# Expert rows fetched one chunk early into the combine of a two-layer encoder; the last chunk's rows added by TensorE

## The reference

```
x = LN(ALPHA * x + Mix(x))      # conv module, windowed attention, gMLP; shared input and output projection
x = LN(ALPHA * x + MoE(x))      # 16 SwiGLU experts (1024 -> 512 -> 1024), top 2 of the best of 4 groups
```

```
for e in range(N_EXPERTS):
    he = silu(x2d @ w_gate[e]) * (x2d @ w_up[e])
    y = y + gates[:, e:e + 1] * (he @ w_down[e])
```

## Time and profile before

| what | value |
|---|---|
| median of 3 runs | 1137.98 us |
| profiled execution, its own time | 1142.18 us |
| its span in the trace | 1140.4 us |
| mean granted TensorE clock | 0.918 |
| busy: TensorE, VectorE, ScalarE, GpSimd | 965.8, 807.7, 648.9, 521.6 us |
| DMA moved | 268.99 MB |

### The profile page before, as it was taken

How to read it: one execution, slowest core, us unless ns; L and a number is a source line. 1 busy time by engine, 2 the same in 40 slices (tenths; PEclk the granted TensorE clock), 3 DMA queues, 4 the chain that set the end, 5 groups by cost and what they waited for, 6 DMA issues and landing times. The chain is left out here.

```text
span 1140.4 us, 15102 instructions
## 1 busy us (share of the span) xinstructions
PE 965.8 (85%) x4700; PEld 780.4 (68%) x4700; DVE 807.7 (71%) x964; ACT 648.9 (57%) x723; POOL 521.6 (46%) x297
## 2 busy tenths in 40 slices
PE   4998998289999999999269979982899999999950
PEld 3866775168888887878268757751688888888840
DVE  2996755567778787777467967555677787878737
ACT  4224712078878887877213347120788787878730
POOL 3435354035656556565205453440356565564621
PEclk9998998679999999999679989986799999999985
DMA  8521183079999999963713211930799999999625
GB/s 271 187 81 39 57 331 147 1 263 360 373 368 366 381 355 371 364 264 108 227 38 111 74 46 51 336 146 3 265 373 378 370 357 372 352 370 367 255 114 143
DMA packets 122511, 268.99 MB, mean 236 GB/s; under 512 B 10608, under 2 KB 26128, under 8 KB 121968
## 3 DMA queue, kind: packets, MB, share of 16 engines
q1 hardware_dynamic: 110192, 243.99, 59.0%
q0 software_dynamic: 12288, 24.60, 6.7%
HBM read 263.38 MB, written 24.64 MB: 253 GB/s over the span
## 5 line engine op out<-in xcount | busy, mean ns | idle before, releaser
L1500 POOL TENSOR_TENSOR wl<-w_down,wh 128x2048 fp32r<-128x2048 f32 x33 | 151.6, 4595 | 165.5 <-ACT wh L937 165.5
L1026 DVE TENSOR_TENSOR wl<-w_gate,wh 128x2048 fp32r<-128x2048 f32 x71 | 166.0, 2339 | 58.3 <-ACT wh L937 30.4
L1026 DVE TENSOR_TENSOR wl<-w_up,wh 128x2048 fp32r<-128x2048 f32 x66 | 151.2, 2293 | 29.5 <-ACT wh L937 29.1
L702 PE MATMUL bank<-wh,xTh 128*128 128x512 f32 x528 | 143.4, 394 | 4.5 <-ACT wh L937 4.5
L937 ACT ACTIVATE wh<-w_down 128x2048 fp32r<-128x2048 f32 x66 | 126.8, 1921 | 30.0 <-PE bank L702 30.0
L702 PE MATMUL bank<-wh,xTl 128*128 128x512 f32 x528 | 142.8, 393 | 0.0
L702 PE MATMUL bank<-wl,xTh 128*128 128x512 f32 x528 | 142.8, 393 | 0.0
L937 ACT ACTIVATE wh<-w_up 128x2048 fp32r<-128x2048 f32 x66 | 126.5, 1917 | 25.5 <-PE bank L720 24.9
L1444 POOL TENSOR_TENSOR wl<-w_gate,wh 128x2048 fp32r<-128x2048 f32 x17 | 78.0, 4593 | 135.5 <-ACT wh L794 135.2
L1026 DVE TENSOR_TENSOR xTl<-bank,xTh 128x512 fp32r<-128x512 f32 (+1 forms) x168 | 89.9, 574 | 62.5 <-ACT xTh L941 24.7
L396 PE MATMUL bank<-xTh,wh 128*128 128x512 f32 (+2 forms) x272 | 112.2, 412 | 24.9 <-DVE xTl L1026 21.1
(11 more groups left out here) (206 smaller groups left out, 1726.5 us busy)
## 6 DMA issues: line engine op xcount, KB each, us to landing
w_up<-in_exp_w_up SPq DMA_DIRECT2D x32, 2048.0 KB, 13.3
w_down<-in_exp_w_down SPq DMA_DIRECT2D x32, 2048.0 KB
w_gate<-in_exp_w_gate SPq DMA_DIRECT2D x32, 2048.0 KB, 12.6
w_gate<-in_w_in SPq DMA_DIRECT2D x14, 1024.0 KB, 5.5
w_gate<-in_w_out SPq DMA_DIRECT2D x8, 1024.0 KB, 5.0
x_rows<-xtok POOLq DMA_DIRECT2D x8, 512.0 KB, 3.0
w_gate<-in_rows_mix SPq DMA_DIRECT2D x2, 1536.0 KB, 6.3
w_up<-in_x_t SPq DMA_DIRECT2D x4, 512.0 KB, 7.5
```

The costliest lines, as they stand in the source:

```text
L702: mm = pe.matmul(bank[piece][:, :], xgT[m][:, 4 * (i % 2) + k, :], w[q][:, k, :], start=(i % 2 == 0 and n == 0 and k == 0), stop=(i % 2 == ...
L1026: return dve.tensor_tensor(out, src, high.bitcast(F32), ALU.subtract)
L1500: pool.tensor_tensor(wl[s][:, :], slot[r][p][:, cols], wh[s][:, :].bitcast(F32), ALU.subtract)\
```

## The change

- Both DRAM buffers `yd` are filled with zeros once: SP issues 16 stores of 512 KB from a zeroed tile (`zero_choices`) behind piece 9 of the first layer, and GpSimd waits for them before the first gather.
- The last chunk's result is not scattered. `load_choices` waits only for the scatter issued within the last chunk's iteration; rows that the last chunk would have written are read as zeros. It fetches both choices for tiles 0 and 1, and GpSimd adds the second choices of tiles 2 and 3 only. In the transition it stands ahead of the mixer's parameters on SP.
- VectorE builds a table of the last chunk (`hot_last`): for each slot of the chunk and each token of a tile, one where the slot's token is that token, else zero. It joins x and the fetched rows (`join`), and TensorE adds in PSUM the identity times the joined tile and the table times `ysb` (`add_choices`): per tile four plain float32 products of 128x128 by 128x512.
- The norm's statistics and its first product read PSUM (`norm_ffn`); the last product is done by ScalarE (scale) and GpSimd (shift) for tiles 0 and 2 in the transition and tiles 0 to 2 at the end, by VectorE for the others. GpSimd takes the power of tile j + 1 ahead of the shift of tile j.
- In the transition ScalarE makes the high parts of pieces 0 and 1 ahead of the last `result`, each as soon as its slot is free; the slots are shifted by one in the second layer so that the right ones are free. `turn` uses other banks and no longer waits for low parts.

The diff, cut to the changed lines and a little around them; left out are the declarations of semaphores, the further places where the slot index changes in the same way, and the rename of the call of `norm`:

```diff
@@ -158,6 +158,8 @@
         cve, crs = small[:, 36:40], small[:, 40:44]
+        last_tok = small[:, 44:45]
+        last_hot = sg
         bnm = [small[:, 112 + 12 * j:124 + 12 * j] for j in range(TT)]
@@ -259,7 +262,11 @@
-            return bank[4 + 2 * (j % 2) + i] if q % 2 else bank[4 * i + j]
+            return bank[2 * j + i] if q % 2 else bank[4 * i + j]
+        def shifted(l, ffn):
+            return (0, 2) if ffn and l + 1 < DEPTH else (0, 1, 2)
@@ -307,14 +314,21 @@
-                end = first_chunk(sp, l, E)
-                sp.wait_ge(split_done[1], end)
-                sp.wait_ge(split_done[2], end)
-                sp.wait_ge(scattered, (end + (l + 1)) * 16)
+                last, end = first_chunk(sp, l, E - 1), first_chunk(sp, l, E)
+                sp.wait_ge(scattered, end * 16)
+                sp.wait_ge(split_done[1], last)
+                sp.wait_ge(split_done[2], last)
                 y = yd[l].rearrange("(r j p) n -> j p r n", r=2, p=P)
                 for j in range(TT):
-                    n = 1 if j else 2
+                    n = 1 if j >= 2 else 2
                     sp.dma_start(ycomb[j][:, 0:n, :], y[j][:, 0:n, :]).then_inc(y_in[j], 16)
+            def zero_choices():
+                sp.wait_ge(pool_chain, 1)
+                for l in range(DEPTH):
+                    for r in range(8):
+                        sp.dma_start(yd[l][P * r:P * r + P, :], xg).then_inc(y_zeroed, 16)
@@ -334,13 +348,15 @@
                     load_piece(l, 1)
+                    load_choices(l - 1)
                     sp.wait_ge(split_done[2], first_chunk(sp, l - 1, E))
                     mix_params(l)
-                    load_choices(l - 1)
                 for q in range(2, PIECES):
...
                     load_piece(l, q)
+                    if q == 9 and l == 0:
+                        zero_choices()
                     if q == 4 and l == 0:
@@ -629,8 +645,6 @@
                 pe.wait_ge(ln_out, TT * q + j + 1)
-                if q % 2 and j >= 2:
-                    pe.wait_ge(tr_low, 2 * (TT * q + j - 1))
                 for k in range(KD):
@@ -742,6 +756,18 @@
                 narrow(l, c, 5)
+            def add_choices(l, j, end):
+                pe.wait_ge(xc_set, TT * l + j + 1)
+                for h in range(2):
+                    pe.matmul(bank[2 * j + h][:, :], ident, xtok[:, j, 512 * h:512 * h + 512], start=True, stop=False)
+                pe.wait_ge(last_set, l + 1)
+                pe.wait_ge(y_set, end + (l + 1))
+                for h in range(2):
+                    mm = pe.matmul(bank[2 * j + h][:, :], last_hot[:, P * j:P * j + P], ysb[:, 512 * h:512 * h + 512],
+                                   start=False, stop=True)
+                mm.then_inc(y_added, 1)
@@ -771,6 +797,9 @@
                     chunk(l, c)
+                end = first_chunk(pe, l, E)
+                for j in range(TT):
+                    add_choices(l, j, end)
@@ -996,14 +1025,24 @@
                     hidden_high(end, l, i)
+                if l + 1 < DEPTH:
+                    act.wait_ge(half_used, halves_done(end, 1, 1))
+                    piece(l + 1, 0)
+                    act.wait_ge(half_used, halves_done(end, 1, 1) + 1)
+                    piece(l + 1, 1)
                 result(end, l, 1)
                 if l + 1 < DEPTH:
-                    for n in range(2):
-                        piece(l + 1, n)
-                    for j in range(TT):
-                        columns_high(2 * l + 1, j)
+                    scaled(2 * l + 1, 0)
+                    columns_high(2 * l + 1, 0)
+                    columns_high(2 * l + 1, 1)
+                    scaled(2 * l + 1, 2)
+                    columns_high(2 * l + 1, 2)
+                    columns_high(2 * l + 1, 3)
                     piece(l + 1, 2)
+                else:
+                    for j in range(TT - 1):
+                        scaled(2 * l + 1, j)
@@ -1128,21 +1167,15 @@
                 dve.wait_ge(piece_high, n + 1)
-                low(wl[n % SLOTS][:, :], wraw[n % 2], wh[n % SLOTS][:, :]).then_inc(piece_low, 1)
+                low(wl[(n + l) % SLOTS][:, :], wraw[n % 2], wh[(n + l) % SLOTS][:, :]).then_inc(piece_low, 1)
...
-                    dve.wait_ge(y_in[j], 16 * (l + 1))
-                    if j:
-                        dve.wait_ge(y_joined[j - 1], 16 * (l + 1))
-                    link(dve.scalar_tensor_tensor(xtok[:, j, :], xtok[:, j, :], ALPHA, ycomb[j][:, 0, :],
-                                                  ALU.mult, ALU.add))
-                    if j == 0:
-                        link(dve.tensor_tensor(xtok[:, j, :], xtok[:, j, :], ycomb[0][:, 1, :], ALU.add))
-                    norm_stats([xtok[:, j, 0:512], xtok[:, j, 512:1024]], j, 2)
+                    dve.wait_ge(y_added, TT * l + j + 1)
+                    norm_stats([bank[2 * j][:, :], bank[2 * j + 1][:, :]], j, 2)
                 else:
@@ -1165,19 +1198,49 @@
-            def norm(l, ffn):
-                dve.wait_ge(rows_in, 32 * l + (32 if ffn else 16))
+            def join(l, j):
+                dve.wait_ge(y_in[j], 16 * (l + 1))
+                if j >= 2:
+                    dve.wait_ge(y_joined[j - 2], 16 * (l + 1))
+                x = dve.scalar_tensor_tensor(xtok[:, j, :], xtok[:, j, :], ALPHA, ycomb[j][:, 0, :], ALU.mult, ALU.add)
+                if j < 2:
+                    link(x)
+                    x = dve.tensor_tensor(xtok[:, j, :], xtok[:, j, :], ycomb[j][:, 1, :], ALU.add)
+                x.then_inc(xc_set, 1)
+            def hot_last(l):
+                at = dve.value_load(starti[0:1, bass.ds(l * (E + 1) + E, 1)], min_val=1, max_val=MAXCH - 1)
+                link(dve.tensor_copy(last_tok, toki[:, bass.ds(at - 1, 1)]))
+                iota = cst[:, K_IOTA:K_IOTA + P]
                 for j in range(TT):
-                    norm_in(l, j, ffn)
-                    if ffn and l + 1 < DEPTH and j >= 1:
-                        columns_low(2 * l + 1, j - 1)
+                    x = dve.tensor_scalar(last_hot[:, P * j:P * j + P], iota, float(P * j), last_tok,
+                                          ALU.add, ALU.is_equal)
+                x.then_inc(last_set, 1)
+            def norm_mix(l):
+                dve.wait_ge(rows_in, 32 * l + 16)
+                for j in range(TT):
+                    norm_in(l, j, 0)
                     dve.scalar_tensor_tensor(xtok[:, j, :], xtok[:, j, :], mv[:, 2 * j:2 * j + 1],
-                                             rows3[:, 0 if ffn else 1, :], ALU.subtract, ALU.mult).then_inc(ln_norm, 1)
-                    if ffn or j == TT - 1:
-                        norm_out(l, j, ffn)
-                    if not ffn and j >= 2:
+                                             rows3[:, 1, :], ALU.subtract, ALU.mult).then_inc(ln_norm, 1)
+                    if j == TT - 1:
+                        norm_out(l, j, 0)
+                    if j >= 2:
                         columns_low(2 * l, j - 2)
+            def norm_ffn(l, j):
+                norm_in(l, j, 1)
+                for h in range(2):
+                    c = slice(512 * h, 512 * h + 512)
+                    x = dve.scalar_tensor_tensor(xtok[:, j, c], bank[2 * j + h][:, :], mv[:, 2 * j:2 * j + 1],
+                                                 rows3[:, 0, c], ALU.subtract, ALU.mult)
+                x.then_inc(ln_norm, 1)
+                if j not in shifted(l, 1):
+                    norm_out(l, j, 1)
@@ -1405,12 +1468,12 @@
                 n = PIECES * (l + 1) - 1
-                low(wl[n % SLOTS][:, :], wraw[n % 2], wh[n % SLOTS][:, :]).then_inc(last_low, 1)
+                low(wl[(n + l) % SLOTS][:, :], wraw[n % 2], wh[(n + l) % SLOTS][:, :]).then_inc(last_low, 1)
                 for j in range(TT):
...
                     add_mix(l, j, 0)
-                norm(l, 0)
+                norm_mix(l)
                 dve.wait_ge(wr_high, l + 1)
@@ -1420,12 +1483,25 @@
                     hidden_low(end, l, i)
+                hot_last(l)
+                join(l, 0)
                 if l + 1 < DEPTH:
...
                         piece_lows(l + 1, q)
-                norm(l, 1)
+                dve.wait_ge(rows_in, 32 * l + 32)
+                join(l, 1)
+                join(l, 2)
+                norm_ffn(l, 0)
+                join(l, 3)
+                norm_ffn(l, 1)
                 if l + 1 < DEPTH:
-                    columns_low(2 * l + 1, TT - 1)
+                    columns_low(2 * l + 1, 0)
+                    columns_low(2 * l + 1, 1)
+                norm_ffn(l, 2)
+                norm_ffn(l, 3)
+                if l + 1 < DEPTH:
+                    columns_low(2 * l + 1, 2)
+                    columns_low(2 * l + 1, 3)
@@ -1441,27 +1517,42 @@
                 pool.wait_ge(piece_high, n + 1)
-                pool.tensor_tensor(wl[n % SLOTS][:, :], wraw[n % 2], wh[n % SLOTS][:, :].bitcast(F32), ALU.subtract)\
```

(40 more changed lines are left out.)

## The result

| | before | after |
|---|---|---|
| median of 4 runs (lowest to highest) | 1138.62 us (1137.33 to 1140.45) | 1123.45 us (1121.37 to 1126.02) |
| profiled execution, its own time | 1142.18 us | 1121.37 us |
| its span | 1140.4 us | 1119.6 us |
| mean granted clock | 0.918 | 0.943 |
| end of the last product to the end of VectorE, second layer | 35.5 us | 22.3 us |

The changed kernel is faster: ratio 0.9867, 95% interval 0.984 to 0.9893, that is 15.2 us of 1138.62 (12 to 18). The forecast was 1120, its range 1114 to 1130.

What follows compares the result with a forecast made beforehand. TensorE bounds the chunk loops; only the two tails with TensorE idle, 35.5 and 31.5 us, can be won from. Savings 12.3 + 5.7 = 18.0 us from 1142.18 give 1124.2; the median, 4.2 lower, 1120; range 1114 to 1130.

Steps and rivals of the forecast that it cites:

- Fetches one chunk early: Both tails: fetches start once the last chunk but one's scatter lands, at 1088.8 instead of 1105.0, and at 541.2.
- Adding DMAs: Both tails: two instead of three, taking 5.5 and 6.8 us at the end, 8.8 and 10.5 between the layers.
- Rivals 2 and 3: Adding DMAs land late, 1126 us, chance 0.12; or before VectorE needs them, 1115.5 us, chance 0.10.
- The norm from PSUM: Expert norms in both tails: 3.5 us a tile plus 1.25, so 4.75 instead of 5.85 us.
- rival 2: Adding DMAs late, 12.2 us between the layers and 8.4 at the end: 1126 us, chance 0.12.
- Rival 5: Early fetch hidden by the norm chain and PSUM reads cost more: 1133 to 1138 us, chance 0.04.
- End of VectorE: Second layer's end: last VectorE instruction 22.7 us after the last product instead of 35.5.
- TensorE's adds: Both tails: four products per tile, 3.4 us at full clock, 6.8 at half; no norm waits for them.
- Rival 1: TensorE's adds run at half clock throughout, 6.8 us a tile, and become the bound: 1132 us, chance 0.12.
- Tile 2 and the projection: Between the layers: tile 2 leaves GpSimd at 582.3, first 48 products end at 582.4, neither waits long.
- The zeros: First layer: 16 stores, 8.4 MB, take 42 us at most and cost nothing; bound 28 us.
- rival 4: Zero writes hold the piece behind them on SP's queue; at 100 GB/s 28 us lost, 1148 us, chance 0.04.

Runs made afterwards that it cites:

- The experiment in the kernel before: Kernel before, only the second layer's last norm product shared out (ScalarE scales, GpSimd shifts tiles 0 to 2), norm still from SBUF: 1142.58 us, ratio 1.0038.

## Why the prediction was right

- **Fetches one chunk early.** Forecast 10.7 us ahead of the last product's end (1088.8 against 1099.5), measured 10.7. The scatters landed in 3.5 and 7.3 us as in the earlier trace rows. The late fetch took the whole gain away (8.8 and 12.3 us).
- **Adding DMAs.** At the end 5.5 was taken from the earlier trace rows, 5.38 came. Between the layers 8.8 was taken from the earlier trace rows, and this is the term that was mis-sized: the DMA for tile 2 took 9.02 us in the first profile, and 9.60, 9.82, 9.91, 10.28 and 10.41 in the five others with the same transition; the tails are 26.2, 26.7, 27.0, 27.0, 27.6 and 27.6. The tail follows the landing nearly one to one. Over these six profiles it is 27.0 on average, so this part gained 4.6 us, not 5.7. Rivals 2 and 3 were about this number; what came lies between the forecast and rival 2 (12.2).
- **The norm from PSUM.** Forecast 3.5 us a tile, measured 3.32; the 1.25 beside it is the join (measured 1.22), and what the sharing takes off VectorE is the product of 1.28 us. The experiment in the kernel before shows that this sum was right only because VectorE reads PSUM: with SBUF operands the same sharing lost 3.6 us. The prediction did not have the lock between VectorE and GpSimd at all; it priced each engine's instruction alone, and that this did no harm was luck. Rival 5, that PSUM reads cost more, is refused by the 3.32.
- **End of VectorE.** Forecast 22.7 us behind the last product, measured 22.3, with the wait for GpSimd's last shift in it, as forecast.
- **TensorE's adds.** Forecast 3.4 us a tile at full clock, measured 3.44, and no norm waited. Half clock for tile 1 between the layers came as forecast, for its first two products. Rival 1 is refused for this kernel, but the doubled adds show how near it stands: 2 us of cover.
- **Tile 2 and the projection.** Forecast out of GpSimd 34.2 us behind the last product, measured 34.3 (578.82 against 544.5). The first 48 products ran partly at full clock and took 7.5 us instead of 8.4, so the transposes of tile 2 waited 0.6 us for GpSimd.
- **The zeros.** Cost nothing, as forecast, with far more room than the bound had it: rival 4 would have needed a rate below 113 GB/s, and 416 was seen. The deadline was misread, as told above, to the safe side. The small copies beside the stores, for which the prediction gave nothing, did land late: GpSimd's two of 90 to 92 us took 5.9 and 6.1 us instead of 2.4 and 2.3, and the next cast, at 116.4 (116.1 before), shows no loss from it beyond the scatter.
- **What was left out.** The second layer's chunk loop, which the change does not touch, got 1.2 to 1.7 us longer; moving it by sixteen instructions gave 0.8 back, so most of this, if not all, is its place in VectorE's program. With it the sum over the stretches is 4.6 + 13.2 - 0.4 - 1.3 = 16.1 us, inside the measured 12 to 18, where 18.0 was forecast. The remaining microsecond can't be told from the scatter: the second mixing half, from projection to the start of the chunk loop, took 212.6 to 219.1 us over the profiles.

## What to carry to other kernels

Ask of every tail which of its transfers depends on the last piece of work at all: here all rows but those of the last chunk, at most 128 of 1024, were ready 16 us before they were fetched (1088.8 against 1105.06), and a small table product adds the rest. An accumulating DMA is slow and shares badly, and became the last to end; but fetching one of its two parts plainly won only 0.6 us at one place and at most 0.9 at the other, since the longer fetch delays the adding DMA that is left. Before work is shared between VectorE and GpSimd, look at where VectorE's operands lie: with two in SBUF it stands still for nearly as long as GpSimd's instruction runs, with one in PSUM its times did not change.

## What the runs showed of the hardware that was not expected

- VectorE with two SBUF operands and a GpSimd add on SBUF exclude each other: VectorE 3.37 and 3.36 us instead of 1.23, 2.65 instead of 1.22, 2.41 instead of 1.28, each ending some 1.1 us after GpSimd's instruction.
- The first adding DMA of 512 KB took 5.3 to 5.6 us at the end, with no weights beside it, and 9.0 to 10.7 beside two weight pieces, while four plain fetches, 3.15 MB together, were done 10 us after the first was issued.
- A long row of 512 KB stores from SP slows SP's own issuing (the last 16 of 48 took 21.25 us to issue, the 16 of the changed kernel 13.95) and moves 416 GB/s, though a single one lands no sooner than 2.6 us.
- The turn of the same loop on VectorE took 1.38, 1.52 or 1.61 us, and 1.61 became 1.52 when only its place in the program changed.
